# One weight stream from the Hyena output to the experts, with the router inside it, and two-part moving operands in the Hyena data projections

## The chip, the cores and the metric

The kernel runs on one core of one Trainium2 chip. The metric is the device time of one execution in microseconds (us). The kernel before took 2426.45 us (median of three runs, 2424.12 to 2429.18).

## The reference, cut to what matters

One layer over 256 latent tokens and 256 context tokens of 2048 channels, all in float32: a modulated RMSNorm, one wide input projection, two parallel token mixers (SSD and Hyena), a gated merge of both, an output projection with a residual, then a second modulated RMSNorm and a two-level mixture of experts.

```
u3 = short_conv(p[..., COL_HY:COL_GATE], hy_conv_w, hy_conv_b)      # 3 taps, rows of 64 tokens
v, x1, x2 = split(u3, 3)
z2 = x1 * fft_long_conv(v, kf[:, 0], bias0);  y_hy = x2 * fft_long_conv(z2, kf[:, 1], bias1)
gates = sigmoid(p[..., COL_GATE:] + gate_b)
merged = gates[..., :D] * (y_ssd @ w_ssd_out) + gates[..., D:] * (y_hy @ w_hy_out)
x = x + gt1 * (merged @ w_o)
h = modulate(rmsnorm(x, norm2_g), sh2, sc2)
g_logits = h @ w_rg + b_rg                   # 4 groups: the best one, its softmax weight
e_logits = h @ w_re + b_re                   # 16 experts: the best two inside the group
x = x + gt2 * sum_e combine[e] * (silu(h @ w_gate[e]) * (h @ w_up[e])) @ w_down[e]
out = rmsnorm(x, final_g)
```

## The kernel before, in words

**Exact products from rounded parts.** The matmuls on the big weights run on a float32 type that TensorE rounds. So each operand is split into a rounded part (`hi`) and the rest (`lo = value - hi`), and each product is three matmuls into one accumulator (`mm3`, lines 195 to 197): hi x hi, hi x lo, lo x hi. The normed tokens `h_hi`, `h_lo` hold two sets of 256 columns (latent tokens at index 0, context tokens at 1).

**The weight stream.** Weights come in slabs of 128 x 1024 numbers (512 KB). SyncE (SP) loads them into a ring of 8 raw slots (`raw`, `load`, L156). For each slab, in the order of the stream, ScalarE (ACT) rounds it into one of four slots of `w_hi` (`split_hi`, L185) once TensorE (PE) has used the slab four places before, VectorE (DVE) subtracts to get `w_lo` (`split_lo`, L189), and PE takes the slab when `lo_ready` has counted it. Each engine runs its own instructions in the order in which they are written, so whatever stands before a split in ACT's or DVE's program delays the splits behind it.

**Blocks.** Each `nc.Block()` ends with a barrier of all engines. The stages around the change:

1. The branch block (phases 4 to 6, 192 slabs, 606 to 1357 us): the z gate, the SSD output projection, then 31 steps `project(b)` of four slabs each. Steps 0 to 23 are the Hyena data projections: each makes two tiles of 128 channels x 256 tokens in two PSUM banks; ACT's `copy_out(b)` brings them into `pad` and DVE's `conv(b)` runs the three taps. Between the steps PE has the plain float32 matmuls of the spectral convolution (filters, spectrum, forward, inverse). Steps 24 to 30 are gate projections.
2. `gated_projection` (phase 7, 64 slabs, 1357 to 1547 us): a loop of 8 rounds of 8 slabs, four of the gate columns on `h` and four of `w_hy_out` on the Hyena output `ys`; sigmoid on ACT, `merge` on DVE (L1214, L1220).
3. The output projection (phase 9, 32 slabs, 1547 to 1660 us): `merged` is split into `ys_hi`, `ys_lo`, then 4 rounds of 8 slabs into the same two PSUM banks; `residual(i)` on DVE (L1880, L1885) reads them, and PE waits for that read before the next round (`s.read`).
4. The expert block (phases 10 to 12, from 1660 us). First, with no expert slab in use: squares and root of the norm (L2231, L2233), `h2` from `x` (L2331, L2333), 16 times transpose, copy, split and router logits (L2072, L2339, L2236, L2341, L2064), some forty tiny DVE operations that pick the groups, the placement matrices `pick` (L2410), 16 gathers of the picked tokens (L2090, float32, 320 columns), each split by ACT and DVE (L2241, L2242, L2417, L2419), and the expert weights. The first expert's slabs are loaded as soon as its group is known (`s.first`). Then PE goes through `order`: 8 gate slabs of expert 0, then its up slabs mixed with the gate slabs of expert 1 (whose tokens are the picked ones), and so on, 384 slabs in all.

GpSimd (POOL) issues the small loads of each block through its own queue.

Of the kernel before, what the change touches and what calls it, by code (L numbers as in the profile page):

```python
# [21 lines left out]
P = 128  # L22
# [113 lines left out]
class Stream:  # L136


    def __init__(self, k, sem):
        self.k, self.done = k, 0  # L140
        self.full = [sem(f"raw_full{s}") for s in range(RAW)]
        self.slots_free = sem("slots_free")
# [18 lines left out]
    def feed(self, sp, iters, per, src, used, following):  # L161
# [3 lines left out]
        def one(i, last):  # L165
            for j in range(per):
# [3 lines left out]
                sp.sem_inc(self.slots_free, 1)  # L170
# [29 lines left out]
def build(nc, io, consts):  # L200
    ctx = ExitStack()
    with ctx:
# [33 lines left out]
        k.h_hi = place("h_hi", [P, 2, KT, L], F32R)  # L236
        k.h_lo = place("h_lo", [P, 2, KT, L], F32R)
# [918 lines left out]
        def gated_projection(phase, half, src, following):  # L1156

            g = place(f"p{phase}_g", [P, 2, L], at=low)
            prod = place(f"p{phase}_prod", [P, 2, L], at=after(f"p{phase}_g"))
            s = Box()  # L1160
            s.gated, s.merged = sems(
                f"p{phase}", "gated", "merged")
            with nc.Block() as block:

                @block.sync
                def _(sp):
                    st.feed(sp, 8, 8, src, st.lo_ready, following)

                @block.tensor
                def _(pe):  # L1170
                    with pe.Fori(0, 8) as i:
                        for j in range(8):
                            if j == 0:
                                pe.wait_ge(s.gated, i + 1)
                            if j == 4:
                                pe.wait_ge(s.merged, i + 1)
                            pe.wait_ge(st.lo_ready, i * 8 + j + 1 + st.base)
                            for c in range(2):
                                for kk in range(4):
                                    kt = 4 * (j % 4) + kk  # L1180
                                    a = ((k.h_hi[:, 0, kt, :], k.h_lo[:, 0, kt, :]) if j < 4 else
                                         (k.ys_hi[:, kt, :], k.ys_lo[:, kt, :]))
                                    cols = slice(c * P, (c + 1) * P)
                                    mm = mm3(pe, k.psum[2 * (j // 4) + c][:, 0:L],
                                             (st.hi(j, 4)[:, kk, cols], st.lo(j, 4)[:, kk, cols]), a,
                                             kt == 0, kt == KT - 1)
                            mm.then_inc(st.w_used, 1)
# [1429 lines left out]
```

## Time and profile before

| | us |
|---|---|
| median of three runs | 2426.45 |
| the profiled execution | 2423.98 |
| its span, first to last instruction | 2422.4 |
| PE busy | 2219.8 (92%) |
| DVE busy | 1507.7 (62%) |
| ACT busy | 1026.5 (42%) |
| DMA, mean over the span | 208 GB/s |

The span is the time from the first to the last instruction of the profiled execution; the time of the execution holds 1.6 us more. "Busy" is time in which an engine has an instruction in flight. Consecutive matmuls overlap in the records: a row's duration is longer than the distance to the next row's start, and it is this distance (the pitch) that a stream of matmuls costs.

### The profile page before, as it was taken

What the parts mean: (1) busy time and instruction counts of PE and PEld (TensorE: products, weight loads), DVE (VectorE), ACT (ScalarE), POOL (GpSimd) and SP (SyncE); (2) the same over time, 40 slices, a digit from 0 to 9 for tenths busy, and PEclk for the clock granted to TensorE, in tenths of its full rate; (3) what the DMA queues carried; (4) which work ended last, traced back from release to release, by engine and by line L of the source; (5) the groups of instructions that cost most, each with busy time, mean ns of one, the idle gap of its engine ahead of it and who ended that gap; (6) DMA issues with size and microseconds to landing.
All of it is one profiled execution on the core that took longest, in us unless ns stands there. A gap on an engine that the chain in (4) does not pass through costs nothing. (4 is left out here: it accounts for less than half of the span.)

```text
span 2422.4 us, 33953 instructions
## 1 busy us (share of the span) xinstructions
PE 2219.8 (92%) x12605; PEld 1799.4 (74%) x12605; DVE 1507.7 (62%) x2013; ACT 1026.5 (42%) x1309; POOL 105.7 (4%) x119
## 2 busy tenths in 40 slices
PE   5789998998899999999999999985799999999995
PEld 0278886454789987888888999865688888778784
DVE  1355555565464466777775444544566776899997
ACT  2433332211464433333333344422355555677774
POOL 1000000000000002020201000000000000000000
PEclk9889999999899999999999999996799999999997
DMA  9833324999567654343443466640378888899993
GB/s 365 341 88 92 92 86 149 337 338 339 172 193 227 184 147 134 109 127 109 138 124 114 148 181 182 242 148 23 133 258 268 279 285 266 290 363 386 359 354 144
DMA packets 301790, 503.57 MB, mean 208 GB/s; under 512 B 18757, under 2 KB 158576, under 8 KB 299878
## 3 DMA queue, kind: packets, MB, share of 16 engines
q1 hardware_dynamic: 296694, 481.54, 59.3%
q0 software_dynamic: 4976, 20.43, 2.4%
q8 instruction: 75, 1.23, 0.2%
q14 instruction: 45, 0.37, 0.0%
HBM read 499.78 MB, written 2.13 MB: 207 GB/s over the span
## 5 line engine op out<-in xcount | busy, mean ns | idle before, releaser
L189 DVE TENSOR_TENSOR w_lo<-raw,w_hi 128x1024 fp32r<-128x1024 f32 x720 | 875.3, 1236 | 548.9 <-ACT w_hi L185 525.5
L185 ACT ACTIVATE w_hi<-raw 128x1024 fp32r<-128x1024 f32 x720 | 751.6, 1058 | 755.0 <-PE bank L197 730.9
L195 PE MATMUL bank<-h_hi,w_hi 128*128 128x256 f32 (+1 forms) x1664 | 514.5, 309 | 29.1 <-DVE w_lo L189 29.1
L196 PE MATMUL bank<-h_lo,w_hi 128*128 128x256 f32 (+1 forms) x1664 | 507.7, 305 | 0.0
L197 PE MATMUL bank<-h_hi,w_lo 128*128 128x256 f32 (+1 forms) x1664 | 507.7, 305 | 0.0
L195 PEld LDWEIGHTS bank<-h_hi,w_hi 128*128 128x128 f32 x1664 | 320.9, 193 | 46.6 <-issue 29.5
L196 PEld LDWEIGHTS bank<-h_lo,w_hi 128*128 128x128 f32 x1664 | 320.8, 193 | 14.4 <-issue 1.9
L197 PEld LDWEIGHTS bank<-h_hi,w_lo 128*128 128x128 f32 x1664 | 320.5, 193 | 13.0
L263 PE MATMUL bank<-raw,cpad 128*32 128x512 f32 x768 | 149.5, 670 | 23.6 <-DMA raw<-in_ada_w 23.6
L195 PE MATMUL bank<-w_hi,ys_hi 128*128 128x512 f32 x384 | 153.6, 400 | 17.8 <-DVE p_tmp L1880 11.4
L196 PE MATMUL bank<-w_lo,ys_hi 128*128 128x512 f32 x384 | 152.7, 398 | 0.0
L197 PE MATMUL bank<-w_hi,ys_lo 128*128 128x512 f32 x384 | 152.3, 397 | 0.0
L195 PE MATMUL bank<-ys_hi,w_hi 128*128 128x256 f32 x512 | 145.0, 283 | 0.0
L196 PE MATMUL bank<-ys_lo,w_hi 128*128 128x256 f32 x512 | 144.9, 283 | 0.0
L197 PE MATMUL bank<-ys_hi,w_lo 128*128 128x256 f32 x512 | 144.9, 283 | 0.0
L263 PEld LDWEIGHTS bank<-raw,cpad 128*32 128x32 f32 x768 | 25.9, 118 | 116.9 <-DMA raw<-in_ada_w 76.8
L195 PE MATMUL bank<-w_hi,mt_hi 128*128 128x512 f32 x256 | 101.3, 396 | 5.1 <-DVE w_lo L189 4.9
L195 PE MATMUL bank<-w_hi,hidt_hi 128*128 128x512 f32 x256 | 101.5, 397 | 4.3 <-DVE hidt_lo L2489 2.6
L197 PE MATMUL bank<-w_hi,hidt_lo 128*128 128x512 f32 x256 | 100.4, 392 | 0.0
L196 PE MATMUL bank<-w_lo,hidt_hi 128*128 128x512 f32 x256 | 100.3, 392 | 0.0
L195 PEld LDWEIGHTS bank<-w_hi,ys_hi 128*128 128x128 f32 x384 | 74.2, 193 | 34.7 <-issue 14.2
L197 PE MATMUL bank<-w_hi,mt_lo 128*128 128x512 f32 x256 | 99.8, 390 | 0.0
(403 smaller groups left out, 3079.9 us busy)
## 6 DMA issues: line engine op xcount, KB each, us to landing
raw<-in_w_in SPq DMA_DIRECT2D x240, 512.0 KB, 3.9
raw<-in_ada_w SPq DMA_DIRECT2D x192, 512.0 KB, 8.1
raw<-in_moe_w_gate SPq DMA_DIRECT2D x128, 512.0 KB, 5.0
raw<-in_moe_w_up SPq DMA_DIRECT2D x128, 512.0 KB, 5.7
raw<-in_moe_w_down SPq DMA_DIRECT2D x128, 512.0 KB, 5.8
raw<-in_w_ssd_out SPq DMA_DIRECT2D x32, 512.0 KB, 4.6
raw<-in_w_hy_out SPq DMA_DIRECT2D x32, 512.0 KB, 3.5
raw<-in_w_o SPq DMA_DIRECT2D x32, 512.0 KB, 3.7
```

The costliest lines, as they stand in the source:

```text
L185: act.activation(self.k.w_hi[:, j % HL, :], self.k.raw[:, j % RAW, :], ACT.Copy).then_inc(self.hi_ready, 1)
L189: dve.tensor_tensor(self.k.w_lo[:, j % HL, :], self.k.raw[:, j % RAW, :], self.k.w_hi[:, j % HL, :].bitcast(F32), ALU.subtract).then_inc(s ...
L195: pe.matmul(out, lhs[0], rhs[0], start=start, stop=False)
L196: pe.matmul(out, lhs[0], rhs[1], start=False, stop=False)
L197: return pe.matmul(out, lhs[1], rhs[0], start=False, stop=stop)
L263: mm = pe.matmul(bank[32 * strip:32 * strip + 32, :], k.cpad[:, kt, :], w[:, 0, n * 512:(n + 1) * 512], start=(kt == 0), stop=(kt == KT - 1))
```

## The change

**Hyena data projections.** `h_hi` and `h_lo` become the two halves of one tile `h_both`. For steps 0 to 23, `project(b)` issues two matmuls per weight tile in place of three: w_hi against the rounded and the rest tokens side by side (512 columns, a whole PSUM bank), then w_lo against the rounded tokens (256 columns). The second half of the bank then holds the hi x lo product, and `conv(b)` adds it into `pad` with two more DVE operations.

**One block from phase 7 on.** `gated_projection`, the output projection and the experts become one block with one stream: slabs 0 to 63 (`WO0 = 64`), 64 to 95 (`MOE0 = 96`), then the 384 expert slabs, all written out in place of the loops of phases 7 and 9. At the start of the block PE waits for seven POOL loads (`s.in_c`, 112): modulation rows and norm gain as 16 x 128 rows, the router weights and biases. It turns the rows into columns `cc`; DVE makes router weights scaled by the modulation and a bias term. The output projection alternates between two pairs of banks.

**The router on raw tokens.** After round i of the output projection, PE transposes the new columns of `x` (`turn_x`) and takes router logits of them inside round i + 1; the norm's factor per token is applied to the logits afterwards. ACT sums squares per round. `h2` is gone: `ys_hi`, `ys_lo` are made per channel tile from the kept transposes (`token_scaled`, `token_highs`, `token_lows`), the gathers read `x` with a scaled placement matrix `pickr`, and ACT applies scale and shift when it reads them (`gx`).

**Gathers between the first expert's gate slabs.** Before gate slab q of expert 0 PE does gathers 2q and 2q + 1; ACT and DVE split their results before they split slab q. The expert weights (`group_weights`, `expert_weights`, `second_exp`) come behind the split of up slab 2, the transposes of `pick` behind up slab 5 on PE, and `way_back` behind up slab 7.

```diff
                 def project(b):
                     if b >= 2:
+                        pe.wait_ge(s.summed, min(b - 1, 24))
+                    if b > 25:
                         pe.wait_ge(s.padded, b - 1)
...
+                            bank = k.psum[2 * (b % 2) + c]
+                            for kk in range(4 if b < 24 else 0):
+                                kt = 4 * q + kk
+                                cols = slice(c * P, (c + 1) * P)
+                                mm = pe.matmul(bank[:], st.hi(j, 4)[:, kk, cols], h_both[:, :, 0, kt, :],
+                                               start=(kt == 0), stop=False)
+                                mm = pe.matmul(bank[:, 0:L], st.lo(j, 4)[:, kk, cols], k.h_hi[:, 0, kt, :],
+                                               start=False, stop=(kt == KT - 1))
...
                 def conv(b):
                     dve.wait_ge(s.padded, b + 1)
+                    for c in range(2):
+                        x = rows_of(pad[:, c, :])[:, :, 2:2 + GRID_W]
+                        ins = dve.tensor_tensor(x, x, rows_of(k.psum[2 * (b % 2) + c][:, L:2 * L]), ALU.add)
+                    ins.then_inc(s.summed, 1)
+                    dve.wait_ge(s.summed, b + 1)
...
# POOL, first in the new block
+                for n, src in enumerate((k.ada_rows[D:2 * D], k.ada_rows[2 * D:3 * D], io["norm2_g"][0])):
+                    pool.dma_start(rows8[n * KT:(n + 1) * KT, :], src.rearrange("(r m) -> r m", m=P)).then_inc(s.in_c, 16)
+                pool.dma_start(wr[:, :, 0:MG], wview(io["moe_w_rg"][0])).then_inc(s.in_c, 16)
+                pool.dma_start(wr[:, :, MG:], wview(io["moe_w_re"][0])).then_inc(s.in_c, 16)
+                pool.dma_start(br[:, 0:MG], io["moe_b_rg"][0].partition_broadcast(P)).then_inc(s.in_c, 16)
+                pool.dma_start(br[:, MG:], io["moe_b_re"][0].partition_broadcast(P)).then_inc(s.in_c, 16)
...
# PE
+                pe.wait_ge(s.in_c, 112)
+                pe.transpose(k.psum[4][:, 0:3 * KT], rows8[0:3 * KT, :], k.tri[0:3 * KT, 0, 0:3 * KT]).then_inc(s.turned, 1)
+                for n in range(WO0):
...
+                    if n == 24:
+                        pe.wait_ge(s.wrs, 1)
+                        for kt in range(KT):
+                            mm = pe.matmul(k.psum[5][:, 0:MG + EXPERTS], k.ones, wrb[:, kt, :], start=(kt == 0),
+                                           stop=(kt == KT - 1))
...
+                for n in range(WO0, MOE0):
+                    i, j = (n - WO0) // 8, n % 8
+                    if j == 0 and i >= 2:
+                        pe.wait_ge(s.read, i - 1)
...
+                    if i and j == 3:
+                        turn_x(i - 1)
+                    if i and j == 5:
+                        logits(i - 1)
+                turn_x(3)
+                logits(3)
...
+                def gather(kt):
+                    if kt >= 2:
+                        pe.wait_ge(s.gx, kt - 1)
                     for t in range(TT):
+                        mm = pe.matmul(k.psum[6 + kt % 2][:, 0:MID + SM], k.x[:, t, kt * P:(kt + 1) * P], pickr[:, t, :],
                                        start=(t == 0), stop=(t == TT - 1))
                     mm.then_inc(s.picked, 1)
...
                     if kind == GATE:
+                        if e == 0:
+                            gather(2 * q)
+                            gather(2 * q + 1)
+                            pe.wait_ge(s.lo, 2 * q + 2)
...
# ACT
+                def keep_xt(i):
+                    act.wait_ge(s.turned, i + 2)
+                    for c in range(2):
+                        ins = act.activation(xt8[:, 4 * i + 2 * c:4 * i + 2 * c + 2, :].rearrange("p a n -> p (a n)"),
+                                             k.psum[c][:], ACT.Copy)
...
+                def picked_highs(kt):
+                    act.wait_ge(s.picked, kt + 1)
+                    if kt >= 2:
+                        act.wait_ge(s.lt_lo, kt - 1)
+                    own_gx = act.activation(gx[:, kt % 2, :], k.psum[6 + kt % 2][:, 0:MID + SM], ACT.Identity,
+                                            bias=cc[:, kt:kt + 1], scale=cc[:, KT + kt:KT + kt + 1])
+                    own_gx.then_inc(s.gx, 1)
+                    act.wait_ge(s.gx, kt + 1)
+                    act.activation(mt_hi[:, kt, :], gx[:, kt % 2, 0:MID], ACT.Copy)
+                    act.activation(lt[:, kt, 0:SM], gx[:, kt % 2, MID:MID + SM], ACT.Copy).then_inc(s.lt_hi, 1)
...
+                for n, (kind, e, q) in enumerate(order, MOE0):
+                    if kind == GATE and e == 0:
+                        for kt in (2 * q, 2 * q + 1):
+                            token_highs(kt)
+                            picked_highs(kt)
                     st.split_hi(act, 0, 0, n)
+                    if kind == UP and e == 0 and q == 2:
+                        second_exp()
...
# DVE
+                for t in range(TT):
+                    ins = dve.tensor_scalar(pickr[:, t, :], pick[:, t, 0:MID + SM], rstd[:, t:t + 1], None, ALU.mult)
...
+                for n, (kind, e, q) in enumerate(order, MOE0):
+                    if kind == GATE and e == 0:
+                        if q == 0:
+                            token_scaled(0)
+                        for kt in (2 * q, 2 * q + 1):
+                            if kt + 1 < KT:
+                                token_scaled(kt + 1)
+                            token_lows(kt)
+                            picked_lows(kt)
                     st.split_lo(dve, 0, 0, n)
+                    if kind == UP and e == 0 and q == 2:
+                        group_weights()
+                        expert_weights()
+                    if kind == UP and e == 0 and q == 7:
+                        way_back()
```

## Rows read from the trace of the kernel before

**Rows 1.** The page, busy time, share of the span and instructions of PE.

```profile
PE 2219.8 (92%) x12605; PEld 1799.4 (74%) x12605; DVE 1507.7 (62%) x2013; ACT 1026.5 (42%) x1309; POOL 105.7 (4%) x119
```

**Rows 2.** Busy time of each engine by stage, then granted clock, DMA share, GB/s.

```profile
907.00:1343.00 436.00, 417.41 (x2764) 355.08 (x2765) 304.96 (x409) 149.44 (x189) 62.77 (x49) 1.00 0.40 122
1357.00:1546.00 189.00, 186.07 (x1536) 185.87 (x1536) 87.87 (x86) 73.22 (x80) 0.00 (x0) 0.99 0.59 178
1550.00:1657.00 107.00, 94.88 (x384) 76.69 (x384) 49.97 (x52) 35.31 (x37) 0.87 (x2) 0.93 0.48 175
1657.00:1739.00 82.00, 45.26 (x188) 36.28 (x188) 49.84 (x155) 25.37 (x61) 5.61 (x16) 0.65 0.21 68
1739.00:1763.00 24.00, 23.55 (x98) 19.41 (x99) 12.29 (x11) 8.83 (x9) 0.00 (x0) 0.93 0.67 219
```

**Rows 3.** Timeline of PE in a Hyena projection: start, duration, then the instruction.

```profile
1055.06 0.28 PE L195 MATMUL bank<-h_hi,w_hi 128*128 128x256 f32 x1
...
1059.73 0.28 PE L195 MATMUL bank<-h_hi,w_hi 128*128 128x256 f32 x1
```

**Rows 4.** Timeline of PE in the z projection, 512 columns.

```profile
654.94 0.39 PE L195 MATMUL bank<-w_hi,h_hi 128*128 128x512 f32 x1
...
659.47 0.39 PE L197 MATMUL bank<-w_hi,h_lo 128*128 128x512 f32 x1
```

**Rows 5.** Timeline of DVE: convolution, the inverse's reader, a merge of phase 7.

```profile
1042.12 1.67 DVE L1700 SCALAR_TENSOR_TENSOR p_v<-p_pad,vcol,p_v 128x256 f32<-128x256 f32 x4
1045.60 1.66 DVE L1770 SCALAR_TENSOR_TENSOR p_x<-bank,small,p_x 128x256 f32<-128x256 f32 x4 [1.82 <-PE bank L1461]
...
1545.77 0.76 DVE L1214 TENSOR_TENSOR p_prod<-bank,p_g 128x256 f32<-128x256 f32 x2 [9.28 <-PE bank L197]
```

**Rows 6.** Timeline of ACT and PE at the start of phase 7.

```profile
1357.22 3.90 ACT L185 ACTIVATE w_hi<-raw 128x1024 fp32r<-128x1024 f32 x4 [1.33 <-PEq L1268]
1359.59 0.39 PE L195 MATMUL bank<-h_hi,w_hi 128*128 128x256 f32 x1 [4.58 <-DVE w_lo L189]
```

**Rows 7.** Start of the expert block: timeline of ACT and POOL.

```profile
1659.87 1.91 ACT L2231 ACTIVATE h<-x 128x2048 f32<-128x2048 f32 x1 [12.94 <-PEq L1833]
1660.29 0.53 POOL L2041 DMA_DIRECT2D p_g<-in_norm_g  x1 [109.42 <-POOLq L1833]
1663.67 0.56 POOL L2045 DMA_DIRECT2D p_br<-in_moe_b_re  x1
```

**Rows 8.** DMA issues of the page: KB each, us from issue to landing.

```profile
p_br<-in_moe_b_re POOLq DMA_DIRECT2D x1, 8.0 KB, 4.6
```

**Rows 9.** Timeline of PE after a round of the output projection.

```profile
1578.22 0.54 PE L195 MATMUL bank<-w_hi,ys_hi 128*128 128x512 f32 x1 [3.79 <-DVE p_tmp L1880]
...
1581.94 0.39 PE L195 MATMUL bank<-w_hi,ys_hi 128*128 128x512 f32 x1
```

**Rows 10.** Timeline of PE: small plain float32 matmuls of the Hyena stage.

```profile
1063.09 1.05 PE L1428 MATMUL bank<-tri,p_ktab 128*128 128x1 f32 x8
```

**Rows 11.** The router's logits as a group: busy us, mean ns, idle before.

```profile
L2064 PE MATMUL bank<-p_wr,p_full 128*128 128x20 f32 x64 | 15.4, 366 | 0.3 <-DVE p_full L2339 0.2
```

**Rows 12.** Timeline of the serial stretch: residual, table load, first routing sum.

```profile
1658.06 1.29 DVE L1885 TENSOR_TENSOR x<-x,p_tmp 128x512 f32<-128x512 f32 x2
...
1663.78 1.28 ACT L2233 ACT_TABLE_LOAD   x1
...
1701.77 0.16 DVE L2346 TENSOR_TENSOR router<-bank,p_br 128x4 f32<-128x4 f32 x1 [0.23 <-PE bank L2064]
```

**Rows 13.** Gathers on PE, ACT's readers of them, first matmul of the up stage.

```profile
1713.43 6.76 PE L2090 MATMUL bank<-pick,h 128*128 128x320 f32 x15 [7.73 <-DVEq L2413]
...
1726.33 0.38 ACT L2241 ACTIVATE mt_hi<-bank 128x256 fp32r<-128x256 f32 x1 [0.58 <-PE bank L2090]
1727.41 0.38 ACT L2241 ACTIVATE mt_hi<-bank 128x256 fp32r<-128x256 f32 x1 [0.58 <-PE bank L2090]
...
1768.12 0.39 PE L2115 MATMUL bank<-w_hi,lt 128*128 128x512 f32 x1
```

More of the change, by code:

```diff
@@ L1904, in build @@
[L1904 to L1915 removed]
+        xt8 = place("xt8", [P, KT, L], at=k.where["merged"][0])
+        g7 = place("p7_g", [P, 2, L], at=low)
@@ new lines, in _ @@
+                turn_x(3)
+                logits(3)
+                pe.wait_ge(s.diag, 1)
+                pe.wait_ge(s.read, 4)
+                for t in range(TT):
+                    mm = pe.matmul(k.psum[4][:, t * P:(t + 1) * P], k.ones, diag[:, t, :], start=True, stop=True)
+                mm.then_inc(s.ones_mm, 1)
+                pe.wait_ge(s.picks, 1)
+                pe.wait_ge(s.in_r, 48)
+                tot = k.psum[3]
+                pe.matmul(tot[:, 64:68], k.above, r[:, 0, 16:20], start=True, stop=True)
@@ L2104, in _, with turn_picks @@
-                mm.then_inc(s.weights, 1)
+                def turn_picks():
+                    pe.wait_ge(s.picks, 3)
+                    pe.wait_ge(s.lo, KT)
+                    for q in range(LIGHT):
+                        for t in range(TT):
+                            c = 256 * (q % 2) + t * P
+                            pe.transpose(k.psum[4 + q // 2][:, c:c + P], pick[:, t, q * P:(q + 1) * P], k.ident)
+                    for q in range(LIGHT):
+                        for t in range(TT):
+                            mm = pe.matmul(k.psum[5][:, 256 + 4 * q:260 + 4 * q], pick[:, t, q * P:(q + 1) * P],
+                                           r[:, t, 32:36], start=(t == 0), stop=(t == TT - 1))
+                    mm.then_inc(s.turnp, 1)
@@ new lines, in _ @@
+                for n in range(WO0, MOE0):
+                    i, j = (n - WO0) // 8, n % 8
+                    if i == 0:
+                        act.wait_ge(s.merged, 8)
+                        act.activation(k.ys_hi[:, 2 * j:2 * j + 2, :], k.merged[:, 2 * j:2 * j + 2, :],
+                                       ACT.Copy).then_inc(s.hi9, 1)
+                    st.split_hi(act, 0, 0, n)
+                    if i and j == 5:
+                        squares_of(i - 1)
+                    if i and j == 7:
+                        keep_xt(i - 1)
@@ L2237, in _, with token_highs @@
+                squares_of(3)
+                act.wait_ge(s.norm, 9)
+                act.activation(rms, ms, ACT.Sqrt).then_inc(s.norm, 1)
+                keep_xt(3)
                 act.wait_ge(s.ract, 1)
                 act.activation(r[:, :, 8:12], r[:, :, 0:4], ACT.Exp).then_inc(s.ract, 1)
-                for kt in range(KT):
+                def token_highs(kt):
+                    act.wait_ge(s.full, kt + 1)
+                    act.activation(k.ys_hi[:, kt, :], xs[:, kt % 3, :], ACT.Identity, bias=cc[:, kt:kt + 1]).then_inc(s.hi, 1)
@@ L2349, in wide @@
+                do(ins)
                 def wide(a, n):
```

573 lines of the change are left out of this document (261 added, 312 removed).

## The prediction

> **What bounds the kernel now.** The page first: PE has an instruction in flight for 92% of the span [rows 1], so what counts is PE's stops and what each matmul costs. Then the busy time by stage [rows 2]: in the Hyena stage and the gated projection PE is busy for 417 of 436 and 186 of 189 us at full clock, with DVE at 305 and 88. The output projection has 95 of 107 us. The stretch from 1657 to 1739 has 45 of 82 us, at a mean granted clock of 0.65: there the router's chain over ACT, DVE and PE sets the time. The last view is the timeline at the seams, for what ends each stop.
>
> **Hyena projections.** The stream of 256-column matmuls starts 39 of them in 4.67 us, 0.120 each [rows 3]; that of 512 columns starts 20 in 4.53, 0.2265 each [rows 4]. At 2.4 GHz 256 and 512 columns are 0.107 and 0.213, so each matmul costs 0.013 beyond its columns. A triple costs 0.360 now and 0.2265 + 0.120 = 0.3465 after. There are 24 steps x 4 slabs x 8 = 768 triples: 768 x 0.0133 = 10.2 us less. The columns are the same; only a matmul's fixed part goes.
>
> By the Trainium skill ("TensorE: Matmul & The Clock Gate", Back-to-back issue gap) a warm gap is N / 2.4 + 2.5 ns, so a matmul dropped would give back 2.5 ns, and the term would be an estimated 1.9 us. The rows have five times that, and the measurement goes first.
>
> DVE gets two adds per step, each reading 256 columns from PSUM: 0.76 us a pair [rows 5], some 0.85 with the wait on itself, 20 us in all. I cost them at nothing: after a convolution DVE sat idle 1.82 us until the inverse transform was there [rows 5], and DVE has 131 us unused in this stage [rows 2]. Without that cover it would be at most 8 filter places x 0.85 = 7 us. PE's new wait on `summed` is met before `lo_ready` of the same step, since DVE does the adds ahead of those splits. Term: -10.2 (bounds -12 to 0).
>
> **Start of the new block.** Now PE's first matmul is at 1359.6, 2.4 us after ACT's first split at 1357.22 [rows 6]. After, PE waits for seven POOL loads, and DVE's first split stands behind what PE turns from them. POOL's first issue lay 0.42 us behind ACT's first instruction, and the fifth issue (one short, two of the wide router loads, two biases) came 3.4 us after the first [rows 7]; the new list has two more short ones of 0.53. The last landed 4.6 us after its issue [rows 8]. So 1357.2 + 0.4 + 4.4 + 4.6 = 1366.7. Then the transpose, two tiny DVE operations, two products of 320 columns (about 0.47 each by the 0.38 of 256 columns, rows 5) and the first split: 2.7 us. PE starts at 1369.4, 9.8 us later; nothing covers this, since PE is what bounds phase 7. Bounds +7 to +12. ACT's four splits wait there, ready.
>
> Behind slab 24 PE gets 16 plain float32 matmuls of 20 columns. One such matmul is two records (64 for 32 [rows 11]), and eight records of the smallest kind took 0.92 us to the next instruction [rows 10]: 16 x 2 x 0.115 = 3.7. Term +3.7.
>
> **Output projection.** The seam to it stays: PE must end, then merge, ys split, weight split; only the barrier goes, -0.3. Between rounds PE sat idle 3.79 us until DVE had read the banks, three times, and came back at 1.2 GHz: nine matmuls took 3.72 us from 1578.22 to 1581.94 [rows 9] where full clock takes 2.04, so 1.7 more. With two pairs of banks both go: 3 x (3.8 + 1.7) = 16.5. Three turns (8 transposes, 0.9) and three logit groups (8 matmuls, 1.9) are added in the stream at 2.8 us each, 8.4. `keep_xt` is two PSUM reads in two slabs' time. Term -8.1; bounds -10 to -5.
>
> **Router, from the end of the last output matmul (T) to the end of expert 0's gate slabs.** Before: T = 1656.6. The up stage's first l slab starts at 1768.12 [rows 13], behind two u slabs of 12 x 0.2265, so the gate slabs end at 1762.7: 106.1 us.
>
> After: DVE has `x` at T + 2.8 (1658.06 + 1.29 [rows 12]). PE turns it, cold, by T + 4.7. ACT has meanwhile two squares of 512 columns (0.75 each, a quarter of 1.91 [rows 7] and the accumulator read), a table load of 1.28 [rows 12], the root, and two copies: T + 7.0. Logits at the low clock: 8 x 0.39 = 3.1, so T + 10.2. From there the old chain repeats: from 1701.77 [rows 12] to the first gather at 1713.43 [rows 13] 11.66 us, plus two scaled placements of 0.47: first gather at T + 22.9. Two tiles are gathered at the low clock, 2 x 2.13 = 4.3.
>
> Now the loop over eight gate slabs. In program order, gather 2q + 1 stands on PE behind the matmuls of slab q - 1, and its readers on ACT and DVE stand ahead of the split of slab q, for which PE waits. So nothing runs ahead, though the ring has four places. One turn is in series: two tiles gathered, 2 x 1.08 (1727.41 - 1726.33 [rows 13]); ACT sees the end and does `gx`, waits on itself, `mt_hi`, `lt`, about 1.3 until it may round; rounding, subtracting and start of PE 2.35 (1359.59 - 1357.22 [rows 6]); 12 matmuls, 2.72. That is 8.5 us at full clock, with PE idle 3.65. The nearest row for that stop is 3.79, which ended at the low level three times in three [rows 9], at 1.7 us. So I take 10.2 a turn. The first slab starts at T + 22.9 + 4.3 + 3.6 = T + 30.8; seven turns, 71.4; the last slab 4.4: T + 106.6. Against 106.1: +0.5. The chain ahead of the first gather shrinks from 56.8 us (1656.6 to 1713.4) to 22.9; gathers and gate slabs grow from 49.3 (to 1762.7) to 83.7 and give it back. At full clock throughout it ends at T + 30.8 + 59.5 + 2.7 = T + 93, a term of -13.
>
> **Up slabs of expert 0.** Six transposes and six small matmuls on PE, +2.0. Behind up slab 2 DVE has some 28 tiny operations (0.2 each) round an exponential on ACT, 6 us, ahead of the split of slab 3; ACT's next split waits for two thirds of it. PE has slabs 0 to 2 and one l slab in hand, 9 us, of which the silu with its table load has used 4: a stop of 2.5 (0 to 4). `way_back` lies in idle time. Term +4.5.
>
> **Sum.** -10.2 + 9.8 + 3.7 - 0.3 - 8.1 + 0.5 + 4.5 = -0.1. Span 2422.3, execution 2423.9. The profiled execution (2423.98) lies 2.5 below the median of the runs, so the median would be 2426. A measurement of this kernel can tell about 0.2%, 4.9 us.
>
> **Rivals.**
>
> (A, the forecast) Savings and the new serial loop cancel: 2426, own range 2419 to 2433. Chance 0.46.
>
> (B) PE's clock stays at its high level in the gate loop, or the stop there is shorter than 3.65, since ACT's reads overlap more than I have it. For it: the longest stretch of work between stops is 4.9 us a turn, and short stops of about 1 us in the Hyena stage left the mean clock at 1.00 [rows 2]. Against it: the three stops of 3.79. Full effect -13.5: 2413. Chance 0.28.
>
> (C) Slower, by the loop: each turn holds 16 to 20 hand-overs between engines, and `token_scaled`, `token_highs` and `token_lows` of the next tile are interleaved with the gathers' readers. If they stand on the path too (0.35 to 0.4 each on ACT and DVE, about 1.1 a turn), the eight turns cost 9 more: 2435. It decides from 0.6 a turn. Against it: DVE's share is done while PE multiplies. Chance 0.16.
>
> (D) The pair does not save what it should: if the wide matmul's two-part operand costs, or a matmul's fixed part is no more than the skill's 2.5 ns, the -10.2 goes to between 0 and -2: 2435. For it: no row here has a two-part moving operand. Against it: rows 3 and 4 have the same fixed part at both widths. By the skill's page as quoted above it would be an estimated 2434. Chance 0.10.
>
> **How the numbers follow.** Faster by over 0.2%: all of B (0.28) and 0.06 of A. Slower: 0.06 of A, 0.14 of C, 0.06 of D. Within: the rest, 0.40. The predicted time is A's, 2426. The range reaches to B's full effect less the overlap of other gains, 2411, and to C's or D's alone with A's own spread, 2438; cases of both signs hold more than half, so A's own range stands above.
>
> **What the profile after would show.** PE: pairs of records, 512 and 256 columns, 0.3465 apart per pair; a stop of about 14 us, not 5, ahead of phase 7, ended by a POOL load; no stops between rounds of the output projection; first gather about 23 us after its end; then eight stops of 3.5 to 3.8 us, ended by `w_lo`, and turns of 10.2 with matmuls of the first gate slab at 0.43 apart. A forecast far off would most likely come from turns of 8.5 or below (B) or near 11.5 (C).

## The result, and the profile after

The changed kernel takes 2433.9 us (median of 20 runs, 2425.2 to 2448.9), the kernel before 2424.3 (20 runs, 2417.5 to 2429.2). The ratio is 1.0035, 95% interval 1.0024 to 1.0047: slower by 0.35%, where 2426 and no change were forecast. One run of all, of the kernel with the small matmuls in the seam, took 4094.8 us at a granted clock of 0.80 and is left out of the medians and ratios. The profiled execution took 2437.26 us, 3.4 above its kernel's median, with a span 13.3 us longer than before (2435.7 against 2422.4). So 3 to 4 us of what the two traces differ by belong to this execution, not to the kernel: the medians differ by 9.6.

The page after, busy time: 731 matmul records fewer on PE than in [rows 1] and yet 8 us more of busy time: some matmuls ran longer, and the clock in the stages below says where. Below it the pair's two lines (busy us, mean ns of one).

```profile
PE 2228.1 (91%) x11874; PEld 1766.6 (73%) x11874; DVE 1521.3 (62%) x2066; ACT 1043.9 (43%) x1347; POOL 104.2 (4%) x119
...
L1327 PE MATMUL bank<-h,w_hi 128*128 128x512 f32 x768 | 277.8, 405 | 0.0
L1329 PE MATMUL bank<-h,w_lo 128*128 128x256 f32 x768 | 216.5, 282 | 0.0
```

Busy time by stage, as in [rows 2]: the branch block to PE's stop, the gated projection, the output projection, and the router with the gate slabs. The figure after the busy times is the granted clock as a share of 2.4 GHz: the gated projection lost a little (0.97, before 0.99), the last stretch stands at 0.74.

```profile
614.30:1349.60 735.30, 713.44 (x4080) 592.84 (x4080) 492.26 (x651) 291.61 (x367) 75.64 (x64) 0.99 0.49 148
...
1362.36:1556.24 193.88, 193.88 (x1568) 193.68 (x1568) 86.53 (x85) 69.51 (x76) 0.76 (x1) 0.97 0.63 191
1561.01:1659.14 98.13, 98.13 (x456) 81.72 (x456) 48.89 (x50) 41.57 (x54) 0.00 (x0) 0.97 0.41 129
...
1659.00:1772.00 113.00, 67.02 (x202) 49.70 (x202) 47.26 (x131) 42.02 (x87) 0.00 (x0) 0.74 0.24 79
```

The same bounds in the kernel before give the branch block 741.80 us with 4848 matmuls:

```profile
613.20:1355.00 741.80, 719.99 (x4848) 635.02 (x4848) 470.75 (x603) 291.59 (x367) 76.98 (x64) 0.99 0.49 147
```

At the start of the block the stop has grown from 4.58 us [rows 6] to 9.87 for the last small load, then a transpose, then 2.58 for the first slab's low part. This is PE's timeline; in brackets the idle time before a row and what ended it.

```profile
1359.44 0.34 PE L1927 MATMUL bank<-tri,p_rows 48*128 48x48 f32 x1 [9.87 <-DMA p_br<-in_moe_b_re]
1362.36 0.58 PE L193 MATMUL bank<-h,w_hi 128*128 128x256 f32 x1 [2.58 <-DVE w_lo L187]
```

The gate slabs of expert 0, PE's timeline again: the first gather, the first matmuls of slabs 0, 2, 3, 4 and 7, and within slab 2 how the 0.23 us between matmuls becomes 0.43 after the first four (their starts are the first column).

```profile
1682.07 4.33 PE L2011 MATMUL bank<-pickr,x 128*128 128x320 f32 x8 [8.54 <-DVEq L2451]
1690.00 0.77 PE L193 MATMUL bank<-w_hi,ys_hi 128*128 128x512 f32 x1 [3.60 <-DVE w_lo L187]
...
1712.44 0.47 PE L193 MATMUL bank<-w_hi,ys_hi 128*128 128x512 f32 x1 [4.03 <-DVE w_lo L187]
1712.75 0.40 PE L194 MATMUL bank<-w_lo,ys_hi 128*128 128x512 f32 x1
...
1713.56 0.63 PE L194 MATMUL bank<-w_lo,ys_hi 128*128 128x512 f32 x1
1713.99 0.63 PE L195 MATMUL bank<-w_hi,ys_lo 128*128 128x512 f32 x1
...
1716.86 2.32 PE L2011 MATMUL bank<-pickr,x 128*128 128x320 f32 x8
1723.20 0.47 PE L193 MATMUL bank<-w_hi,ys_hi 128*128 128x512 f32 x1 [4.02 <-DVE w_lo L187]
...
1733.95 0.77 PE L193 MATMUL bank<-w_hi,ys_hi 128*128 128x512 f32 x1 [4.02 <-DVE w_lo L187]
...
1767.06 0.47 PE L193 MATMUL bank<-w_hi,ys_hi 128*128 128x512 f32 x1 [4.02 <-DVE w_lo L187]
```

Seven turns from 1690.00 to 1767.06 are 77.1 us, 11.0 each (10.48 to 11.96). They differ by the clock and not by the stop, which is 4.02 or 4.03 in all of them. The first two turns, by window:

```profile
1690.00:1700.48 10.48, 6.45 (x21) 4.69 (x21) 3.93 (x10) 3.99 (x9) 0.00 (x0) 0.83 0.19 50
1700.48:1712.44 11.96, 7.94 (x20) 5.72 (x21) 3.92 (x10) 3.99 (x9) 0.00 (x0) 0.75 0.12 44
```

The span's 13.3 us by the forecast's own terms; each measured number is a difference of two starts or ends in the two traces. T is the end of the last output matmul, 1656.7 before and 1659.1 after:

| step | forecast | measured | how |
| --- | --- | --- | --- |
| ahead of the branch block | 0 | +1.1 | its first matmul at 613.2, now 614.3 (610.1 to 615.8 over all profiled kernels) |
| Hyena projections | -10.2 | -6.5 | 741.8, now 735.3 |
| start of the new block | +9.8 | +8.2 | 4.6 from PE's stop to the first matmul, now 12.8 |
| 64 gated slabs | +3.7 | +7.8 | 186.1, now 193.9 |
| seam | -0.3 | 0.0 | 4.8 and 4.8 |
| output projection | -8.1 | -8.1 | 106.25, now 98.13 |
| router to end of gate slabs | +0.5 | +6.4 | T + 106.0, now T + 112.4 |
| up slabs of expert 0 | +4.5 | +4.2 | 30.7 to the matmul that waits for `hidt_lo`, now 34.9 |
| rest | 0 | +0.3 | |

### The profile page after: what moved, and what is told of

It is laid out like the page before. It is cut to its first block and busy times, and to the rows that moved or that the text cites. A ratio compares the mean times of both kernels' runs of the same rounds, so it can differ in the third digit from the quotient of the medians.

```text
span 2435.7 us, 31496 instructions
## 1 busy us (share of the span) xinstructions
PE 2228.1 (91%) x11874; PEld 1766.6 (73%) x11874; DVE 1521.3 (62%) x2066; ACT 1043.9 (43%) x1347; POOL 104.2 (4%) x119
## 5 line engine op out<-in xcount | busy, mean ns | idle before, releaser
L193 PE MATMUL bank<-h,w_hi 128*128 128x256 f32 (+1 forms) x896 | 294.5, 329 | 27.1 <-DVE w_lo L187 27.1
L194 PE MATMUL bank<-h,w_hi 128*128 128x256 f32 (+1 forms) x896 | 291.2, 325 | 0.0
L195 PE MATMUL bank<-h,w_lo 128*128 128x256 f32 (+1 forms) x896 | 291.2, 325 | 0.0
L1327 PE MATMUL bank<-h,w_hi 128*128 128x512 f32 x768 | 277.8, 405 | 0.0
L1329 PE MATMUL bank<-h,w_lo 128*128 128x256 f32 x768 | 216.5, 282 | 0.0
L193 PEld LDWEIGHTS bank<-h,w_hi 128*128 128x128 f32 x896 | 174.3, 194 | 41.0 <-issue 25.8
L194 PEld LDWEIGHTS bank<-h,w_hi 128*128 128x128 f32 x896 | 174.2, 194 | 12.9 <-issue 0.5
L195 PEld LDWEIGHTS bank<-h,w_lo 128*128 128x128 f32 x896 | 173.9, 194 | 12.9
L1327 PEld LDWEIGHTS bank<-h,w_hi 128*128 128x128 f32 x768 | 146.3, 191 | 38.5 <-issue 3.7
L264 PE MATMUL bank<-raw,cpad 128*32 128x512 f32 x768 | 151.5, 682 | 23.0 <-DMA raw<-in_ada_w 22.9
L1329 PEld LDWEIGHTS bank<-h,w_lo 128*128 128x128 f32 x768 | 146.7, 191 | 1.4 <-issue 1.4
```

Source lines behind the costliest of these rows:

```text
L193: pe.matmul(out, lhs[0], rhs[0], start=start, stop=False)
L194: pe.matmul(out, lhs[0], rhs[1], start=False, stop=False)
L195: return pe.matmul(out, lhs[1], rhs[0], start=False, stop=stop)
L264: mm = pe.matmul(bank[32 * strip:32 * strip + 32, :], k.cpad[:, kt, :], w[:, 0, n * 512:(n + 1) * 512], start=(kt == 0), stop=(kt == KT - 1))
L1327: mm = pe.matmul(bank[:], st.hi(j, 4)[:, kk, cols], h_both[:, :, 0, kt, :], start=(kt == 0), stop=False)
L1329: mm = pe.matmul(bank[:, 0:L], st.lo(j, 4)[:, kk, cols], k.h_hi[:, 0, kt, :], start=False, stop=(kt == KT - 1))
```

## The experiments

| kernel | median us | ratio to before | 95% interval |
| --- | --- | --- | --- |
| changed kernel | 2433.9 | 1.0035 | 1.0024 to 1.0047 |
| before, with the pairs only | 2416.8 | 0.9969 | 0.9958 to 0.9979 |
| pairs only, grouped by width | 2417.6 | 0.9964 | 0.9951 to 0.9977 |
| pairs only, parts adjacent | 2417.1 | 0.9972 | 0.9960 to 0.9985 |
| changed, triples kept | 2443.5 | 1.0076 | 1.0062 to 1.0091 |
| changed, inputs' wait behind slab 8 | 2422.6 | 0.9993 | 0.9983 to 1.0004 |
| changed, small matmuls in the seam | 2427.3 | 1.0012 | 1.0001 to 1.0023 |
| changed, stop in the gate loop filled | 2416.7 | 0.9969 | 0.9955 to 0.9983 |
| changed, gathers two tiles ahead | 2386.0 | 0.9837 | 0.9819 to 0.9856 |
| changed, four repairs | 2371.6 | 0.9781 | 0.9765 to 0.9797 |
| four repairs, two stops filled | 2371.6 | 0.9774 | 0.9755 to 0.9793 |

Each ratio is to runs of the kernel before that belong to the same batch (their medians are 2424.1 to 2425.4), so that equal medians can have unequal ratios.

### The gate loop: the stop and the clock apart

```diff
                             gather(2 * q + 1)
+                            for _ in range(4):
+                                pe.matmul(k.psum[5][:], k.ident, xt8[:, 0:2, :].rearrange("p a n -> p (a n)"),
+                                          start=True, stop=True)
                             pe.wait_ge(s.lo, 2 * q + 2)
```

> The changed kernel with four matmuls of 512 f32 columns into a free bank behind the two gathers of each gate slab of expert 0: TensorE has work in the stop, which needs the same time as before. Their results are used by nothing. Theory (of a turn's 11.0 us 1.9 are the low clock that the stop leaves behind, 4.0 the stop): turns of 9.0 to 9.2 us, all matmuls of these slabs at 0.23 us, 13 us less, 2421, ratio 0.998. Rival 1 (the clock is low there for another reason than the stop): matmuls of 0.43 us stay, turns of 11 or, with the extra work in the way, longer, 2434 to 2450. Rival 2 (the clock's part is larger: the chain itself is shorter with TensorE at full speed): turns under 8.5 us.

PE's timeline of one turn; L2127 are the extra matmuls:

```profile
1680.77 0.47 PE L193 MATMUL bank<-w_hi,ys_hi 128*128 128x512 f32 x1 [0.17 <-DVE w_lo L187]
...
1683.59 2.31 PE L2011 MATMUL bank<-pickr,x 128*128 128x320 f32 x8
1685.74 3.60 PE L2127 MATMUL bank<-xt,tri 128*128 128x512 f32 x8
1689.93 0.47 PE L193 MATMUL bank<-w_hi,ys_hi 128*128 128x512 f32 x1 [0.59 <-DVE w_lo L187]
```

The turn is 9.16 us (1680.77 to 1689.93, and the next one the same), no matmul of the slabs is at half speed, and the kernel is 17 us faster than the changed one by the medians, though PE does 64 records more. By the traces 14.8 of it lie in the loop (the gate slabs end at T + 97.6, where the changed kernel has T + 112.4); the rest fits the fall of the clock behind the small matmuls, which this execution does not have (below). So of the 11.0 us 1.84 were the clock, as the theory has it; the chain itself is 9.16 and not the forecast's 8.5. By its parts: 12 matmuls 2.82 (forecast 2.72), two gathers 2.15 (2.16), from there to the next slab 4.19 (3.65). The chain over ACT and DVE was 0.54 us longer than I had it.

ACT's timeline of the same turn shows where. The gathers end at 1685.74 by PE's pitch, and ACT begins to round the slab at 1687.48, 1.74 later, where the forecast had 1.3:

```profile
1685.99 0.49 ACT L2216 ACTIVATE ys_hi<-xs,cc 128x256 fp32r<-128x256 f32 x1
1686.38 0.60 ACT L2222 ACTIVATE gx<-bank,cc 128x320 f32<-128x320 f32 x1
...
1687.48 1.04 ACT L183 ACTIVATE w_hi<-raw 128x1024 fp32r<-128x1024 f32 x1
```

ACT is busy without a break from 1684.87 on, with the readers of the first tile and then with `ys_hi`, which is `token_highs` of the second tile. That one operation holds up the second tile's `gx` by 0.39 us (1685.99 to 1686.38), most of the missing 0.54; another 0.10 is in the rounding, subtracting and start of PE (2.45, forecast 2.35). DVE's `xs` and `ys_lo` don't stand in the way: DVE waits 0.39 for the rounded slab before it subtracts. No run moved `token_highs` away, so this is read from the rows and not tested.

### The gate loop: gathers ahead

```diff
                 pe.wait_ge(s.picks, 2)
+                gather(0)
+                gather(1)
                 for kind, e, q in order:
                     if kind == GATE:
                         if e == 0:
-                            gather(2 * q)
-                            gather(2 * q + 1)
+                            if q < 7:
+                                gather(2 * q + 2)
+                                gather(2 * q + 3)
                             pe.wait_ge(s.lo, 2 * q + 2)
```

> The changed kernel with TensorE's gathers two k-tiles ahead: gathers 0 and 1 stand ahead of the loop and gathers 2q+2 and 2q+3 ahead of gate slab q, where the changed kernel has 2q and 2q+1. ScalarE's and VectorE's orders stay. Theory (each turn of 11.0 us is TensorE's work of 5.04, a stop of 4.02 for the chain gather to low part, and cold matmuls for the rest; the stop is there only since the gather stands right before its slab): turns of 5.0 to 5.4 us, no stops over 0.5 us, clock 1.0, 40 us less, 2393, ratio 0.986. Rival (ScalarE and VectorE are the bound of the loop, by their waits on each other, whatever TensorE's order): turns of 8 to 10 us, 2415 to 2428.

```profile
1698.04 2.31 PE L2011 MATMUL bank<-pickr,x 128*128 128x320 f32 x8
1699.95 0.63 PE L193 MATMUL bank<-w_hi,ys_hi 128*128 128x512 f32 x1
1700.42 0.40 PE L194 MATMUL bank<-w_lo,ys_hi 128*128 128x512 f32 x1
```

No stop stands in brackets. Turns are 4.88 us (slabs at 1690.2, 1695.1, 1700.0, 1704.8), PE alone sets them, and busy time by window confirms it with a clock of 1.00; one stop of 1.30 is left, ahead of slab 7, which has no gathers before it:

```profile
1686.00:1718.00 32.00, 31.75 (x131) 24.29 (x129) 25.34 (x61) 26.59 (x60) 0.00 (x0) 1.00 0.42 115
```

The time is 48 us under the changed kernel's, more than the 40 expected. Seven turns give 43 (77.1, now 33.6), and by the traces the gate slabs end 45.5 sooner after T (T + 66.9 for T + 112.4). ACT is busy for 26.6 and DVE for 25.3 of these 32 us, so they were not the bound. With PE's order alone changed, the stops and the half-speed matmuls behind them are gone.

### The start of the block

```diff
-                pe.wait_ge(s.in_c, 112)
-                pe.transpose(k.psum[4][:, 0:3 * KT], rows8[...], ...).then_inc(s.turned, 1)
                 for n in range(WO0):
...
+                    if n == 8:
+                        pe.wait_ge(s.in_c, 112)
+                        pe.transpose(k.psum[4][:, 0:3 * KT], rows8[...], ...).then_inc(s.turned, 1)
```

On DVE the block from `dve.wait_ge(s.turned, 1)` to `wrb` moves behind `split_lo` of slab 13.

> The changed kernel with the wait for the seven small router inputs, and the transpose behind it, moved on TensorE from before slab 0 to behind slab 8, and VectorE's products of the router weights moved behind its split of slab 13. Theory (the start of the block is nothing but this wait: 12.8 us between the Hyena stage and the first matmul against 4.58 before): the first matmul comes 4.5 to 5 us after the Hyena stage, the time falls by 8 us from 2434 to 2426, ratio to the kernel before 1.000. Rival (the block opens late anyway, by its queues' first transfers or the first slab's splits, and the small inputs were only the last of several): it falls by at most 3, ratio 1.002 to 1.0035.

```profile
1352.85 0.58 PE L193 MATMUL bank<-h,w_hi 128*128 128x256 f32 x1 [4.32 <-DVE w_lo L187]
```

The start is back at 4.3 us, and the whole price of the start is gone. By the medians it is 11 us less. By the traces it is 8.5 of the stop (12.8, now 4.3) and 2.5 of the 64 slabs behind it (193.9, now 191.4), which have 6.6 us at 1.2 GHz and not 13.0.

### The 16 small matmuls

```diff
-                    if n == 24:
-                        pe.wait_ge(s.wrs, 1)
-                        for kt in range(KT):
-                            mm = pe.matmul(k.psum[5][:, 0:MG + EXPERTS], k.ones, wrb[:, kt, :], ...)
-                        mm.then_inc(s.ones_mm, 1)
-                pe.wait_ge(s.wrs, 2)
+                pe.wait_ge(s.wrs, 1)
+                for kt in range(KT):
+                    mm = pe.matmul(k.psum[6][:, 0:MG + EXPERTS], k.ones, wrb[:, kt, :], ...)
+                mm.then_inc(s.ones_mm, 1)
                 pe.wait_ge(s.merged, 8)
```

PE's wait until `s.wrs` is 2 moves to round 1 of the output projection.

> The changed kernel with the 16 f32 matmuls of 20 columns (ones times router weights) moved on TensorE from behind slab 24 into the stop between hyena output and output projection (4.77 us, for the last merge), and VectorE's add of their result behind the split of slab 66. Theory (these matmuls cost their own 3.9 us and, by the clock at half speed from 1440 to 1447 us right behind them, 3.4 more): the 64 slabs take 7.3 us less, 186.5, the seam stays at 4.8, the time falls from 2434 to 2427. Rival (the clock falls there without them too): 3.9 less, 2430, and a stretch of matmuls at half speed stays near 1440.

In the changed kernel's profiled execution they took 3.9 us (to the next slab at 1441.04), and the clock fell right behind them (matmuls of 256 columns 0.21 us apart instead of 0.12):

```profile
1437.16 4.05 PE L1947 MATMUL bank<-p_wrb,tri 128*128 128x20 f32 x32
...
1441.40 0.41 PE L194 MATMUL bank<-h,w_hi 128*128 128x256 f32 x1
1441.61 0.41 PE L195 MATMUL bank<-h,w_lo 128*128 128x256 f32 x1
```

Moved into the seam they lie beside the wait for the last merge: the 64 slabs take 186.8 us instead of 193.9, and the seam, from the last slab's end to the next one's start, is 4.62 (4.77 in the changed kernel).

```profile
1544.87 4.31 PE L1946 MATMUL bank<-p_wrb,tri 128*128 128x20 f32 x32
1549.65 0.77 PE L193 MATMUL bank<-w_hi,ys_hi 128*128 128x512 f32 x1 [0.47 <-issue]
```

The number is the theory's, its mechanism only half: with the small matmuls still behind slab 24, the clock does not always fall there. The changed kernel and the one with triples kept have 6.8 us at 1.2 GHz right behind them, the one with late inputs 3.4, the gathers-ahead and the stop-filled kernel none. The row is the same stretch in the changed kernel, then in the one with gathers ahead:

```profile
1435.00:1455.00 20.00, 20.00 (x146) 20.00 (x145) 7.57 (x9) 5.57 (x7) 0.00 (x0) 0.83 0.45 131
```

```profile
1435.00:1455.00 20.00, 20.00 (x171) 20.00 (x170) 8.80 (x10) 6.25 (x9) 0.00 (x0) 1.00 0.52 156
```

So the matmuls cost 3.5 to 4.0 us each time, and in three of the five profiled executions 1.7 to 3.4 more. The profiled execution of the changed kernel had that bad luck, and it may be why it lies above its own median. What decides it was not tried.

### The pairs

Pairs alone, on the kernel before (project, conv and the shared tile `h` as in the change, nothing else):

> The kernel before with nothing of the change but the pairs of the Hyena data projections (512 columns from both parts, 256 from the low weights) and the adds in the convolution. Theory (the pair costs 0.353 us and not 0.3465, so that 768 of them give back 5.1 us rather than 10.2): the Hyena stage is 5 to 6.5 us shorter than in the kernel before, the time near 2419, ratio 0.9974 to 0.998. Rival 1 (the pairs give the forecast 10.2 us, and something later in the changed kernel's stage took half of it back): 2414, ratio 0.9958. Rival 2 (the adds or the longer hold of the banks cost as much as is saved): ratio 0.999 to 1.001.

The branch block takes 732.5 us against 741.8, the time falls by 7.5 us (5 to 10 by the interval). Averaged over the eight pairs of a slab, two sizes stand in each execution in which the widths alternate: 0.3467 us in about a fifth of the slabs, 0.3525 to 0.354 in most others. First rows of the larger size in the changed kernel (0.355 over the two pairs shown), then of the smaller in the kernel with pairs only (0.345):

```profile
1220.08 0.40 PE L1327 MATMUL bank<-h,w_hi 128*128 128x512 f32 x1
...
1220.44 0.40 PE L1327 MATMUL bank<-h,w_hi 128*128 128x512 f32 x1
...
1220.79 0.40 PE L1327 MATMUL bank<-h,w_hi 128*128 128x512 f32 x1
```

```profile
1008.25 0.39 PE L1412 MATMUL bank<-h,w_hi 128*128 128x512 f32 x1
...
1008.59 0.40 PE L1412 MATMUL bank<-h,w_hi 128*128 128x512 f32 x1
...
1008.94 0.39 PE L1412 MATMUL bank<-h,w_hi 128*128 128x512 f32 x1
```

Over the stage, the mean start-to-start of a pair is about 0.352 us and that of a triple before about 0.361 (stops and half-speed rows left out). That is some 0.0085 for each of the 768, 6.5 us. Neither theory of the expectation has it quite: a pair is dearer than 0.3465, but a triple was dearer than 0.360 too, on the mean, and the rest of the 9.3 in this execution is the clock: by the granted clock it has 7 us less at half speed in this block than the kernel before, worth some 3.5. All twelve profiles agree: the branch block less half of its time at 1.2 GHz is 733.6 us in both kernels with triples, and 726.1 to 727.9 in the ten with pairs, 5.7 to 7.5 less.

To find the missing 0.006, the order by width and the layout:

```diff
+                            for kk in range(4):
+                                mm = pe.matmul(bank[:], st.hi(j, 4)[:, kk, cols], h_both[:, :, 0, kt, :], ...)
+                            for kk in range(4):
+                                mm = pe.matmul(bank[:, 0:L], st.lo(j, 4)[:, kk, cols], k.h_hi[:, 0, kt, :], ...)
```

> The kernel before with the pairs of the Hyena data projections, with each slab's half in another order: four matmuls of 512 columns, then four of 256, where the pairs alternate. Theory A (a pair costs 0.353 us and not 0.3465 in most of the stage because the widths alternate): a half slab of 8 matmuls takes 4 x 0.3465 = 1.386 us, the time is 3 to 5 us under that of the pairs alone, 2412 to 2414. Theory B (it is the two-part operand, or what the other engines and transfers do beside it): half slabs of 4 x 0.353 = 1.41 us, the same time as the pairs alone, 2416 to 2418.

```profile
824.26 1.09 PE L1412 MATMUL bank<-h,w_hi 128*128 128x512 f32 x4
825.19 0.63 PE L1416 MATMUL bank<-h,w_lo 128*128 128x256 f32 x4
825.66 1.09 PE L1412 MATMUL bank<-h,w_hi 128*128 128x512 f32 x4
```

1.40 us per half slab, 0.350 a pair: the 512 columns take 0.232 and the 256 take 0.118. In this order the two sizes are gone: most slabs have 0.351, none has 0.3467. The mean over the stage stays where it was, about 0.352, and so does the time. So the order of the widths decides whether there are two sizes, but not what a pair costs.

```diff
-        h_both = place("h", [P, 2, 2, KT, L], F32R)
-        k.h_hi, k.h_lo = h_both[:, 0], h_both[:, 1]
+        h_both = place("h", [P, 2, KT, 2, L], F32R)
+        k.h_hi, k.h_lo = h_both[:, :, :, 0, :], h_both[:, :, :, 1, :]
```

> The kernel before with the pairs of the Hyena data projections, and the rounded and rest parts of each k-tile side by side in memory: the 512 columns are one run of 2048 bytes in each partition, where they are two runs of 1024, 32 KB apart. Theory A (the two runs cost a pair its 6.5 ns): pairs of 0.3465 us throughout, 2412 to 2414. Theory B (they don't: widths or neighbours): both levels of 0.3465 and 0.353 stay, 2416 to 2418. The f32r splits that write the parts with a stride may cost VectorE or ScalarE up to 1 us, hidden.

The mean pair is about 0.352 us again, both sizes stay, and the time is that of the pairs alone within its interval. So neither the alternation nor the two-part operand makes the pair dearer than 0.3465. That leaves what runs beside it, or which banks and buffers are in use; this stays open. It also disposes of rival D's first reason, the two-part operand.

The complement, triples kept in the changed kernel:

```diff
-                            for kk in range(4 if b < 24 else 0):
+                            for kk in range(0):
...
-                            for kk in range(0 if b < 24 else 4):
+                            for kk in range(4):
```

> The changed kernel with the Hyena data projections as before: three matmuls of 256 columns per k-tile, no adds, the waits on the copies. Theory (the pairs save 0.3607 - 0.3522 = 0.0085 us each, 6.5 in all, and nothing else of the change depends on them): 6 to 8 us slower than the changed kernel, 2441, ratio to the kernel before 1.0065. Rival (the pairs' saving comes with fewer short drops of the clock, or shows only in the kernel before): 2434 to 2437, ratio 1.004 to 1.005.

Its branch block takes 741.8 us, as in the kernel before, and the time is 2443.5, 9.6 above the changed kernel where 6.5 is the stage's share; the intervals of the two ratios leave room for that difference. The adds on DVE and the new semaphore cost nothing that shows in PE's stops, and the pairs are independent of the rest.

### The four repairs together

The three edits above (inputs, small matmuls, gathers), and the expert weights' chain spread over the up slabs:

```diff
-                    if kind == UP and e == 0 and q == 2:
-                        group_weights()
-                        expert_weights()
+                    if kind == UP and e == 0 and q == 0:
+                        group_weights()
+                    if kind == UP and e == 0 and q == 3:
+                        expert_weights()
```

and on ACT `second_exp()` behind up slab 1 instead of 2.

> The changed kernel with four repairs together: the inputs' wait behind slab 8, the 16 small matmuls in the seam, the gathers two k-tiles ahead, and the expert weights' chain split over up slabs 0 to 3 so that ScalarE's exponential does not hold up the splits. If the costs add: gather ahead 2386, less 8 to 11 for the inputs, 6 to 7 for the small matmuls, 1.9 for the stop in the up slabs: 2366 to 2370, ratio 0.976 to 0.978. Rival (the costs overlap: what one repair gains at the start of the block is waited for again at the routing): 2376 to 2380.

```profile
1352.45 0.58 PE L193 MATMUL bank<-h,w_hi 128*128 128x256 f32 x1 [4.32 <-DVE w_lo L187]
...
1538.58 3.65 PE L1947 MATMUL bank<-p_wrb,tri 128*128 128x20 f32 x32
1543.36 0.76 PE L193 MATMUL bank<-w_hi,ys_hi 128*128 128x512 f32 x1 [1.14 <-issue]
...
1671.63 0.47 PE L193 MATMUL bank<-w_hi,ys_hi 128*128 128x512 f32 x1 [0.62 <-DVE w_lo L187]
```

2371.6 us, 2.2% below the kernel before and 62 us below the changed one: it beats both. It is 14.4 under the gathers alone, where 16 to 20 were expected: 8.5 from the start, 3.9 from the small matmuls, 0.7 of the 1.9 in the up slabs, where a stop of 1.18 stays. My expectation had counted the clock's 3.4 behind the small matmuls, which the gathers-ahead kernel did not have in its profile.

Last, two of the remaining stops filled:

```diff
+                for kt in range(16):
+                    for _ in range(2):
+                        pe.matmul(k.psum[6][:, 0:L], k.h_hi[:, 0, kt, 0:P], k.h_hi[:, 0, kt, :], start=True, stop=True)
                 for n in range(WO0):
...
                 pe.wait_ge(s.made, 2)
+                for _ in range(7):
+                    pe.matmul(k.psum[5][:], xt8[:, 0, 0:P], xt8[:, 0:2, :]..., start=True, stop=True)
                 pe.wait_ge(s.picks, 2)
```

> The version with the four repairs, with TensorE given work of no use in two of its stops: 32 matmuls of 256 columns of rounded tokens before gated slab 0 (a stop of 4.6 us), and 7 of 512 f32 columns between the totals and the first gather (8.5 us). Theory (a stop costs its length and, behind it, matmuls at half speed): the first gated slabs and the first gathers run at full speed, 1.7 and 2 to 2.5 us less, 2368, ratio 0.9765; the stops' other ends (w_lo at slab 0, the picks) come no later. Rival (TensorE comes back at the low level whatever it did, or the extra matmuls end later than the data arrives): 2371 to 2374.

```profile
1352.95 0.28 PE L195 MATMUL bank<-h,w_lo 128*128 128x256 f32 x1
1355.15 4.06 PE L1928 MATMUL bank<-h 128*128 128x256 f32 x32 [1.92 <-PEq L1186]
1359.05 0.28 PE L193 MATMUL bank<-h,w_hi 128*128 128x256 f32 x1
1359.17 0.28 PE L194 MATMUL bank<-h,w_hi 128*128 128x256 f32 x1
```

The clock part of the theory holds: the slab behind the filled stop starts at full speed, 0.12 apart. But PE sits idle 1.92 us before the first extra matmul, so the filling ends 1.5 us late (6.1 from the last matmul's start to the slab's instead of 4.6) and eats what it gives (the 64 slabs take 184.9, with four repairs alone 186.3). At the gathers the gain is real: the first gate slab stands 29.3 us behind T instead of 31.1. The time does not show it, 0.9774 against 0.9781, intervals overlapping: no verdict on the whole. The profiled execution is even 4.5 us longer than that of the four repairs, by a stage that the edit doesn't touch: its branch block takes 739.5 us, where that one has 732.6, with 27 us at 1.2 GHz and not 10.

```profile
613.70:1353.20 739.50, 717.68 (x4080) 596.85 (x4080) 491.64 (x651) 291.50 (x367) 73.84 (x64) 0.98 0.48 147
```

## Why the prediction was wrong

**What bounds the kernel**: right. Every term of the table behind the first is a stop of PE, its matmul count, or its clock.

**Hyena projections**: right in kind, mis-sized: -6.5 for -10.2. The price of a pair was put together from one stretch of 39 matmuls of 256 columns in this stage and one of 20 of 512 columns in the z projection. Only about a fifth of the slabs had that price (0.3467); on the mean a dropped matmul gave 8.5 ns, not 13.3. By the Trainium skill ("TensorE: Matmul & The Clock Gate", Back-to-back issue gap) the fixed part is 2.5 ns, a figure that the page gives for an isolated matmul; by it the term would have been an estimated 1.9 us. Stage and triples-kept kernel show more than three times that, so rival D in its form is refuted. The cover for the adds held.

**Start of the new block**: right, +8.2 for +9.8. POOL's seven issues and the last load's landing came 1.5 us sooner than I added up (7.5 from the first issue to the transpose, forecast 9.0). That nothing covers it is shown by moving it away.

**64 slabs**: the 3.7 of the small matmuls measured 3.9 (3.5 to 4.0 over five executions), the stage +7.8. Not foreseen were 3.4 us of clock behind them and, after the longer stop at the start, a longer stretch at half speed (with the small matmuls in the seam the 64 slabs still take 186.8, before 186.1). The first was there in three of five executions.

**Output projection and seam**: right, -8.1 for -8.1, and the seam 0.0 for -0.3. Two pairs of banks removed three stops and their clock, for 98.1 us of unbroken work.

**Router up to the first gather**: right to 0.1 us (T + 22.9, and T + 30.9 for the first slab).

**The gate loop is the step that failed**: "So I take 10.2 a turn." The turns took 11.0, so the term was +6.4 and not +0.5, the largest single miss. The structure was right (in series, stops ended by `w_lo`, half-speed matmuls), and so was the clock's part, 1.84 for 1.7, by the stop-filled kernel. What failed is the sum of 8.5 for the chain: it is 9.16. Its step over ACT ("about 1.3 until it may round") took 1.74, since ACT reads the first tile and does `token_highs` of the second (0.39) before it can turn to the second gather; the rest is 0.1 each for the split and the slab's matmuls. That is a part of what rival C names, one `token_highs` a turn on ACT; DVE's share was hidden, as the argument against C had it. C decides "from 0.6 a turn", and the turns were 0.8 over in all. By these numbers the median would, with 10.2 a turn, have been some 3.7 us above that of before, inside the 0.2%. C at 0.16 was priced too low.

**Up slabs**: +4.2 for +4.5, with a stop of 1.85 rather than 2.5.

**The sum**: misses of +3.7 (pairs), +4.1 (slabs) and +5.9 (loop), with +1.1 ahead of the branch block, stand against -1.6 (start) and -0.3 (up slabs); of the slabs' miss 3.4 is the clock of this execution. With 0.2% as the limit, terms of 10 us each way that cancel can't hold a forecast of no change at 0.40 unless each is known to 2 us; the range of 2411 to 2438 did hold the time, in part because it is wide. The forecast's 2426 also rests on the first three runs of the kernel before; the median of 20 is 2424.3.

## What to carry to other kernels

When gathers or other feeders stand in program order right before the work that needs their result, a merge of two stages turns a pipeline into a chain over three engines; issue them one slab ahead, and look for this before pricing the chain. Here those few lines were worth 48 us, as much as the pairs (6.5), the output projection (8.1) and the shorter chain up to the first gather (33.8: T + 56.7, now T + 22.9) save together. A wait for small inputs belongs at their first use and not at the top of a block: PE stopped 8.2 us longer for values that it needed 24 slabs later. Small matmuls belong in a stop that is there anyway.

## What the runs showed of the hardware

- A stop of 4.0 us on PE left it at 1.2 GHz for part of the next slab in seven turns of seven; the same stop with matmuls in it left 2.4 GHz throughout. The part at half speed cost 1.84 us a turn.
- Thirty-two records of 20-column float32 matmuls, 0.11 to 0.12 us apart without a stop, were followed by 6.8 us at 1.2 GHz in two profiled executions, by 3.4 in one and by none in two, with the same instructions around them.
- Pairs of 512 and 256 columns in turn ran at two sizes, 0.3467 and 0.3525 to 0.354 us averaged over a slab, in every kernel that had them, with either layout of the operand. With four of 512 and then four of 256 most slabs had 0.351, and the mean over the stage was the same.
